# Attention scores of a head's four token tiles in one run, in six banks

## The reference

```python
q, k, v = jnp.split(x @ w_qkv, [qk_dim, 2 * qk_dim], axis=-1)
q = q.reshape(B, S, B_HEADS, 2, B_HEAD_DIM) * (B_HEAD_DIM ** -0.5)
k = k.reshape(B, S, B_HEADS, 2, B_HEAD_DIM)
logits = jnp.einsum('bqhjd,bkhjd->bhjqk', qb, k).astype(jnp.float32)
probs = jax.nn.softmax(logits + bias[:, :, None], axis=-1)
attn = probs[:, :, 0] - lam * probs[:, :, 1]
return jnp.einsum('bhqk,bkhe->bqhe', attn.astype(v.dtype), v)
of = of * lax.rsqrt(jnp.mean(jnp.square(of), axis=-1, keepdims=True) + LN_EPS)
```

## Time and profile before

| what | value |
|---|---|
| device time, median of 3 runs | 1278.77 us (1278.75 to 1279.49) |
| the profiled execution's own time | 1278.82 us |
| its span in the trace | 1277.1 us |
| PE busy | 1266.7 us, 99% of the span |
| DVE, ACT, POOL busy | 51%, 36%, 13% |
| granted TensorE clock, mean | 0.998 |

### The profile page before, as it was taken

The page is one execution under the profiler, slowest core; times in us unless marked ns, Lnnn a source line. Parts: engine busy times, 40 slices in busy tenths (PEclk is TensorE's granted clock), DMA queues, the critical chain, the costliest instruction groups (busy, mean ns, idle before and its releaser), DMA issues.

```text
span 1277.1 us, 15677 instructions
## 1 busy us (share of the span) xinstructions
PE 1266.7 (99%) x6104; PEld 1056.8 (83%) x6104; DVE 650.4 (51%) x889; ACT 459.2 (36%) x553; POOL 164.9 (13%) x159
## 2 busy tenths in 40 slices
PE   9999999999999999999999999999999999999997
PEld 8888888889888888888888877788988888888886
DVE  3637877346343434433372777775653334343346
ACT  3422333322232323322314588775143222232230
POOL 3001100040000000000224444443100000000001
PEclk9999999999999999999999999999999999999999
DMA  8434554250322232222522334324033333322221
GB/s 263 151 96 123 173 175 148 90 183 3 130 99 99 90 101 80 98 92 97 193 71 74 102 100 122 95 104 168 30 99 99 99 99 99 99 99 99 99 99 66
DMA packets 104507, 140.62 MB, mean 110 GB/s; under 512 B 9424, under 2 KB 81192, under 8 KB 104208
## 3 DMA queue, kind: packets, MB, share of 16 engines
q1 hardware_dynamic: 94880, 127.68, 31.0%
q0 software_dynamic: 9440, 12.11, 2.9%
q10 hardware_dynamic: 144, 0.26, 0.1%
HBM read 137.85 MB, written 10.52 MB: 116 GB/s over the span
## 4 chain that ended last, share of the span: by engine, by line
PE 97%; DVE 2%; ACT 0%; issue 0%; POOL 0%; DVEq 0%; POOLq 0%
PE bank L1261 31%; PE bank L1265 31%; PE bank L1264 31%; PE bank L1643 1%; PE bank L1497 1%; PE bank L1271 1%; PE bank L1395 1%; PE bank L1421 0%; DVE x_tok L819 0%; DVE r_stat L788 0%; PE bank L1386 0%; PE bank L1500 0%; DVE x_tok L810 0%; DVE x_tok L782 0%; DVE w_lo L870 0%
## 5 line engine op out<-in xcount | busy, mean ns | idle before, releaser
L1261 PE MATMUL bank<-xt_hi,w_hi 128*128 128x512 f32 (+1 forms) x1008 | 380.8, 378 | 0.0
L1265 PE MATMUL bank<-xt_hi,w_lo 128*128 128x512 f32 (+1 forms) x1008 | 378.8, 376 | 0.0
L1264 PE MATMUL bank<-xt_lo,w_hi 128*128 128x512 f32 (+1 forms) x1008 | 378.7, 376 | 0.0
L760 DVE TENSOR_TENSOR w_lo<-w_raw,w_hi 128x2048 fp32r<-128x2048 f32 x79 | 180.8, 2289 | 184.6 <-ACT w_hi L466 158.3
L1261 PEld LDWEIGHTS bank<-xt_hi,w_hi 128*128 128x128 f32 x1008 | 189.7, 188 | 36.5 <-issue 3.0
L1265 PEld LDWEIGHTS bank<-xt_hi,w_lo 128*128 128x128 f32 x1008 | 189.7, 188 | 34.6
L1264 PEld LDWEIGHTS bank<-xt_lo,w_hi 128*128 128x128 f32 x1008 | 189.8, 188 | 33.7
L466 ACT CAST w_hi<-w_raw 128x2048 fp32r<-128x2048 f32 x53 | 101.2, 1912 | 186.2 <-PE bank L1261 185.1
L1261 PE MATMUL bank<-w_hi,s_hi 128*128 128x512 f32 x416 | 162.2, 390 | 0.6 <-POOL w_lo L1874 0.6
L1265 PE MATMUL bank<-w_hi,s_lo 128*128 128x512 f32 x416 | 161.9, 389 | 0.0
L1264 PE MATMUL bank<-w_lo,s_hi 128*128 128x512 f32 x416 | 161.8, 389 | 0.0
(11 more groups left out here) (209 smaller groups left out, 1490.3 us busy)
## 6 DMA issues: line engine op xcount, KB each, us to landing
w_raw<-in_f_w_in_dram SPq DMA_DIRECT2D x44, 1024.0 KB, 5.1
w_raw<-in_f_w_down_dram SPq DMA_DIRECT2D x22, 1024.0 KB, 4.8
w_raw<-in_a_w_in_dram SPq DMA_DIRECT2D x14, 1024.0 KB, 5.8
bias_by_query_key<-bias_by_distance POOLq DMA_DIRECT2D x8, 1024.0 KB, 15.9
w_raw<-in_a_w_out_dram SPq DMA_DIRECT2D x8, 1024.0 KB, 6.7
w_raw<-in_b_w_qkv_dram SPq DMA_DIRECT2D x16, 512.0 KB, 4.7
bias_sb<-bias_by_query_key SPq DMA_DIRECT2D x32, 256.0 KB, 2.6
w_raw<-in_b_w_qkv_dram SPq DMA_DIRECT2D x4, 1024.0 KB, 5.3
```

Source lines behind the costliest of these rows:

```text
L760: dve.tensor_tensor(lo_of(u), w_raw[:, u % 2, :], hi_of(u), ALU.subtract).then_inc(w_lo_done, 1)
L1261: ins = pe.matmul(o, a_hi, b_hi, start=start, stop=False)
L1264: pe.matmul(o, a_hi, b_lo, start=False, stop=False)
L1265: return pe.matmul(o, a_lo, b_hi, start=False, stop=stop)
```

## The change

It has four parts. PE's scores of a head stand in one run, behind the second transposed pair and the projection's blocks 3 to 5, and all four value blocks stand behind them. The banks of the scores are now 2 and 3, 1 and 4, 5 and 6 (those of the transposes), and 2 and 3 again; so tile 2 waits for DVE's last split of transposed blocks and tile 3, half by half, for the scoring of tile 0. DVE splits the fourth transposed block before any scoring, and scores tile 2 before the first reciprocal and tile 3 before the second. In the last two heads the second value pair stands before the scores, and ACT and DVE take a value block earlier. Head 0 keeps its banks and its order. The core of the diff:

```diff
+        def score_bank(h, t, j):
+
+            if h == 0:
+                return bank[(1, 4)[j] if t % 2 else 2 + j]
+            return bank[((2, 3), (1, 4), (5, 6), (2, 3))[t][j]]
...
             probs_hi(h, 3)
+            values_hi(TB + 2)
             exps(h + 1, 0)
-            values_hi(TB + 2)
...
                 probs_lo(h, 2)
+                probs_lo(h, 3)
                 scored(h + 1, 0)
-                probs_lo(h, 3)
                 scored(h + 1, 1)
+                scored(h + 1, 2)
                 weighed(h + 1, 0)
+                scored(h + 1, 3)
                 weighed(h + 1, 1)
-                scored(h + 1, 2)
                 mixed(h + 1, 0)
-                scored(h + 1, 3)
                 mixed(h + 1, 1)
...
+            for k in range(TB):
+                probs_lo(h, k)
             scored(h + 1, 0)
-            probs_lo(h, 3)
+            values_lo(TB + 2)
             scored(h + 1, 1)
+            scored(h + 1, 2)
             weighed(h + 1, 0)
-            values_lo(TB + 2)
+            scored(h + 1, 3)
             weighed(h + 1, 1)
...
                     elif c == 1:
-                        pe.wait_ge(sc_done, 2 * TB * (h - 1) + 5)
+                        pe.wait_ge(sc_done, 2 * TB * (h - 1) + (5 if h == 1 else 7))
...
+                    else:
+                        pe.wait_ge(sc_done, 2 * TB * h)
+                if t == 2 and h:
+                    pe.wait_ge(at_lo_done, TB * h)
                 for j in range(2):
-                    n = 2 * TB * h + 2 * t + j
-                    if n >= 4:
-                        pe.wait_ge(sc_done, n - 3)
+                    if h == 0 and t >= 2:
+                        pe.wait_ge(sc_done, 2 * t + j - 3)
+                    elif t == 3:
+                        pe.wait_ge(sc_done, 2 * TB * h + j + 1)
...
                 turn_probs(h, 3)
-                scores(h + 1, 0)
-                scores(h + 1, 1)
                 project(h + 2, 0, range(3, 6))
-                values(h, 0)
-                values(h, 1)
-                scores(h + 1, 2)
-                scores(h + 1, 3)
-                values(h, 2)
-                values(h, 3)
+                for t in range(TB):
+                    scores(h + 1, t)
+                for k in range(TB):
+                    values(h, k)
...
-            scores(h + 1, 0)
-            scores(h + 1, 1)
             value_pair(U_V67, 1)
-            scores(h + 1, 2)
-            scores(h + 1, 3)
+            for t in range(TB):
+                scores(h + 1, t)
             value_pair(U_V67, 2)
...
             out_ready(U_BO, S_BO, 0)
-            pe.wait_ge(sc_done, 2 * TB * (H - 1) + 6)
+            pe.wait_ge(sc_done, 2 * TB * H)
```

More of the change, by code:

```diff
@@ L258, in query_key_bank @@
             return bank[2 * c]
-        def score_bank(t, j):
-            return bank[(1, 4)[j] if t % 2 else 2 + j]
+        def score_bank(h, t, j):
+            if h == 0:
+                return bank[(1, 4)[j] if t % 2 else 2 + j]
+            return bank[((2, 3), (1, 4), (5, 6), (2, 3))[t][j]]
         def pair_bank(n):
@@ L1116, in scored @@
                     dve.wait_ge(sc_mm, 2 * TB * h + 2 * t + j + 1)
-                    dve.tensor_tensor_reduce(prob[:, t, j, :], score_bank(t, j)[:, :], bias_sb[:, t, :], -1.0, 3.0e38,
+                    dve.tensor_tensor_reduce(prob[:, t, j, :], score_bank(h, t, j)[:, :], bias_sb[:, t, :], -1.0, 3.0e38,
                                              ALU.add, ALU.min, nmax[:, t, j:j + 1]).then_inc(sc_done, 1)
@@ L1195, in _ @@
             query_key(h + 1, 1)
-            probs_lo(h, 0)
-            probs_lo(h, 1)
-            probs_lo(h, 2)
+            for k in range(TB):
+                probs_lo(h, k)
             scored(h + 1, 0)
-            probs_lo(h, 3)
+            values_lo(TB + 2)
             scored(h + 1, 1)
+            scored(h + 1, 2)
             weighed(h + 1, 0)
-            values_lo(TB + 2)
+            scored(h + 1, 3)
             weighed(h + 1, 1)
-            scored(h + 1, 2)
             mixed(h + 1, 0)
-            scored(h + 1, 3)
             stationary(o_t, S_BO, 0)
@@ L1623, in scores @@
                         pe.wait_ge(bv_lo_done, TB)
+                    else:
+                        pe.wait_ge(sc_done, 2 * TB * h)
+                if t == 2 and h:
+                    pe.wait_ge(at_lo_done, TB * h)
                 for j in range(2):
-                    n = 2 * TB * h + 2 * t + j
-                    if n >= 4:
-                        pe.wait_ge(sc_done, n - 3)
+                    if h == 0 and t >= 2:
+                        pe.wait_ge(sc_done, 2 * t + j - 3)
+                    elif t == 3:
+                        pe.wait_ge(sc_done, 2 * TB * h + j + 1)
                     r = slice(HD * j, HD * j + HD)
                     q = slice(t * P, t * P + P)
-                    product(score_bank(t, j)[:, :], qk_hi[r, h % 2, 0, q], qk_lo[r, h % 2, 0, q],
+                    product(score_bank(h, t, j)[:, :], qk_hi[r, h % 2, 0, q], qk_lo[r, h % 2, 0, q],
                             qk_hi[r, h % 2, 1, :], qk_lo[r, h % 2, 1, :], True, True).then_inc(sc_mm, 1)
```

## The result

The changed kernel takes 1282.7 us (median of 11 runs, 1282.35 to 1283.91) against 1279.01 us for the kernel before in the same session: a ratio of 1.003, with a 95% interval of 1.0022 to 1.0038. It is slower by 0.3%, clear of the 0.2% that was set as the bound of no change. The prediction was 1280.8 us in a range of 1278.4 to 1283.4; the time lies in it, but 0.8 above the forecast's own range (1279.6 to 1281.9). The outcome that I gave most (0.60), no change within 0.2%, did not come; slower by over 0.2%, which had 0.30, did.

A forecast was written before the change was run, and what follows sets the result against it. PE bounds the kernel, its chain covering 97% of the span. From 1278.82 us, +0.9 for the loop (0.46 won, 0.44 lost, then DVE's late queries) and +1.07 for the last heads gave 1280.8 us, range 1278.4 to 1283.4.

The forecast's parts named there:

- 0.46 won against 0.44 lost per head: PE, loop heads: one run of scores saves 0.46 us; tile 3's wait for its second bank loses 0.44.
- Rival (a): Loop: bank free in time, DVE's late start has no follower; 2.8 us won, 1276.0 us; chance 0.10.
- What is late next: Mean of squares: PE arrives at T + 16.27 but sees DVE's lower part of the next queries at 16.33.
- +0.15 per head, 6 x 0.15 = +0.9 us: Loop's six heads: next T at 19.62 against 19.47 through DVE's late queries; bounds 0 to +1.5 us.
- my two terms: Loop, +0.9 us, kept at 0 to +1.5; entry to the output projection, +1.07 us, 0.6 or 1.3 otherwise.
- rival (b): Third reciprocal: POOL's share gets the port before DVE's square split; queries 0.41 later per head, 2.5 us more, 1283.3; chance 0.20.
- The last mix: DVE's fourth mix ends at T + 19.61, before the next head's fourth transpose needs it: covered by 0.25 us.
- The last heads: Output projection: third reciprocal delays POOL's last weight piece, moving PE's entry from 853.66 to 854.73, +1.07 us.
- 1.3 if the split of the heads keeps the share out too: Last heads' bound: 1.3 us instead of 1.07 if DVE's split of the output heads also holds off POOL's share.
- Rival (c): Loop keeps its pace, DVE just in time; only the last heads lose 1.07 us: 1279.9 us; chance 0.20.

The follow-up runs named there:

- the run with bank 7: Changed kernel with tile 0's second half in the values' bank 7, so tile 3's second half has a free bank: 1283.83 us, ratio 1.0037.
- the versions with the other waits gone: Changed kernel with POOL's pieces first, free bank and third reciprocal behind the queries: 1277.05 us; also with the last value block split before the last mix: 1276.62 us.
- the run with the queries early: Changed kernel with only DVE's third reciprocal moved behind the square split and the queries: 1286.04 us, ratio 1.0048.
- The loop-only run: Changed kernel with the old order and old banks in the last two heads, only the loop's six heads changed: 1281.37 us, ratio 1.0019.
- the pieces moved: Changed kernel with POOL's four pieces of weights ahead of the first share in every head: 1279.1 us, ratio 1.0001.

## Why the prediction was right, and where it was off

**PE's saving and the bank wait.** The step that put 0.46 won against 0.44 lost per head holds to a few hundredths: the run starts at T + 5.98 for 5.94, the second half of tile 3 at 8.49 for 8.43, the values end at 12.23 for 12.19. Rival (a), the gain arrives, fell with it; but the run with bank 7 shows that it would have fallen without the bank wait too. The Trainium skill, TensorEngine Tiling (Array Packing), Key Properties, says that changing the tiling mode drains TensorE. The trace agrees that a change costs (0.34 against 0.227), and the versions with the other waits gone have 0.35 of the 0.46 per head. Whether PE is what the head waits for is a second question, and here it decided.

**What is late next.** The place was right: the mean of squares, by way of DVE's queries, and the run with bank 7 names it. Its size was not. The step "+0.15 per head, 6 x 0.15 = +0.9 us" measured 0.40 a head, 2.4 us, above the 0 to 1.5 that I gave it. Three small terms add up. The run and the first scoring came 0.05 later. The second share was done at T + 14.12 instead of 13.98, 0.09 beyond that 0.05; with 0.02 more behind it this put the third reciprocal at 14.83 for 14.67. And PE began 0.15 after DVE's last instruction, where I took the 0.06 that it needed after POOL. Together 0.25, and PE had no slack to take any of it: it was due at 16.31, the queries ended at 16.43, and it began at 16.58. A sum that ends within a tenth of what it must beat carries its whole error into the time.

**That the time lies in the range** is in part luck. The bounds of my two terms, 1.5 for the loop and 1.3 for the last heads, end at 1281.6; the range went on to 1283.4 only to take in rival (b), and (b)'s mechanism is not what filled that room. The loop's own term, priced too low, did, with another 0.2 us ahead of the first head that no change accounts for.

**The last mix** was forecast to be covered, and was: PE shows no wait there in the changed kernel. In the run with the queries early it is what decides.

**The last heads.** The mechanism held; the bound "1.3 if the split of the heads keeps the share out too" was the one that came, and I had taken 1.07. The loop-only run shows the 1.3 by itself.

**Rival (b), the port.** Its sign came, not its mechanism. At the third share the order stayed as before: POOL's share starts 0.07 ahead of the square split and is the one stretched, to 1.23. With the pieces moved, the second share starts 0.07 ahead of a mix (769.79, 769.86) and here the share keeps its 0.69 and the mix waits. The Trainium skill, SBUF — State Buffer, Who interferes with whom, says that who issues first keeps the shared pair for the whole instruction. The second case agrees with it; the first doesn't, and didn't in the kernel before. Both stand in the same head of the same run: the third share starts 0.07 ahead of the square split there too (771.85, 771.92) and takes 1.23. Why, no run here settles. Rival (c), a loop that keeps its pace, fell.

**What stays open**: the cause of the two outcomes at the port; how much of the cost of POOL's old order is the port and how much its queue; how the 0.05 and the 0.09 arise; what PE's order would cost with DVE's old one; and how the one-run saving splits in the last heads, where other waits took its place.

## What to carry to other kernels

When one engine is busy 99% of the time and its slots look improvable, list, for every point at which it takes something from another engine, by how much that something is early. A reordering that frees the busy engine but starts the others' work later spends exactly this slack; here 0.7 us of slack at one point decided, and the point was neither where slots were saved nor where the new wait was added. And two engines that hold each other up are first found in durations: the same instruction at 0.75 and at 1.76 us marks an order of queues that is worth changing if something waits for it. The same move of POOL's pieces took 0.37 us off each head of the changed kernel and nothing off those of the kernel before.

## What the runs showed of the hardware beyond that

In the profiled execution of the run with the queries early alone, 1.55 us of the 1286 are TensorE's clock: from the output projection's first matmul to the values of head 6 it is 4.44 us (859.53 to 863.97), in the changed kernel 2.89 (857.53 to 860.42). Granted clock of two stretches in the last heads (columns: stretch, its length, busy us and instructions of PE, PEld, DVE, ACT, POOL, clock, DMA share, GB/s):

```profile
840.00:859.50 19.50, 17.59 (x137) 16.21 (x135) 13.55 (x33) 11.82 (x24) 8.60 (x7) 1.00 0.08 33
859.50:864.00 4.50, 4.47 (x13) 3.52 (x14) 2.16 (x5) 1.90 (x1) 2.60 (x3) 0.62 0.68 233
```

Behind a wait of 1.94 us for POOL the granted clock fell to the lower of its two levels (2.4 and 1.2 GHz) for about 3 us: from 860.10 to 863.10 it is 0.50. Matmuls of the output projection start 0.43 apart instead of 0.23:

```profile
859.53 0.50 PE L1261 MATMUL bank<-w_hi,s_hi 128*128 128x512 f32 x1 [1.94 <-POOL w_lo L1873]
...
861.01 0.63 PE L1264 MATMUL bank<-w_lo,s_hi 128*128 128x512 f32 x1
...
861.44 0.63 PE L1265 MATMUL bank<-w_hi,s_lo 128*128 128x512 f32 x1
...
863.51 0.39 PE L1264 MATMUL bank<-w_lo,s_hi 128*128 128x512 f32 x1
```

The changed kernel waits 1.91 us at the same place and the run with bank 7 2.2 us, and in their profiled executions the clock stayed at 1.00. Some 20 us earlier PE of this run had been held once more, in the transposes of head 6, whose eight take 1.48 us instead of 0.79; it had been held like that in the heads before too. Without the clock the median would have come to 1284.5, next to the 1285 that was forecast, and two of the five executions did: 1284.53 and 1284.55 us at a mean clock of 0.998 and 0.999, where the other three took 1286.04 to 1286.56 at 0.997. Three of the five executions with bank 7 and one of the eleven of the changed kernel (1283.91 us) also have 0.997 and are 0.9 us or more above the others of their kernel, so the fall seems to come in some executions of each; no trace of those was kept. What tips it isn't settled, and that the wait causes it isn't shown: the one trace that has it shows it right behind a wait of 1.94 us, at a price of 1.55.
